# Modulation rows and summed blocks turned over on TensorE and added up by VectorE

## The reference, cut to what matters

```python
mod = silu(c) @ w_mod[l] + b_mod[l]              # 6 * 1024 values for each of two streams
sh1, sc1, g1, sh2, sc2, g2 = split(mod, 6)
h = rmsnorm(x, norm1_g) * (1 + sc1) + sh1        # first norm
y = token_mixing(h)                              # three mixers, gates, output projection
x = x + g1 * y
h = rmsnorm(x, norm2_g) * (1 + sc2) + sh2        # second norm
x = x + g2 * ec_moe(h)                           # 16 routed experts
```

## Time and profile before

| what | value |
|---|---|
| median of 3 runs | 1779.37 us (1778.21 to 1779.48) |
| span of the profiled execution | 1775.2 us |
| PE busy | 1694.8 us, 95% |
| DVE busy | 647.5 us, 36% |
| ACT busy | 290.4 us, 16% |
| HBM read | 530.76 MB, 300 GB/s over the span |

### The profile page before, as it was taken

One profiled execution on the slowest core, in us unless ns is written; L12 is line 12 of the kernel. 1 busy time (PEld: TensorE's weight loads), 2 busy tenths in 40 slices (PEclk: granted clock), 3 DMA queues, 4 the chain that ended last, 5 costly groups with the idle time before them and its releaser, 6 DMA issues.

```text
span 1775.2 us, 18819 instructions
## 1 busy us (share of the span) xinstructions
PE 1694.8 (95%) x7152; PEld 799.4 (45%) x7152; DVE 647.5 (36%) x1374; ACT 290.4 (16%) x736; POOL 118.6 (7%) x161
## 2 busy tenths in 40 slices
PE   7999999999999998898999999999999998988988
PEld 3456566654434332242345565666553433323322
DVE  1257656566122120121124566666661111211211
ACT  2234222002101010000022432221030100000100
POOL 0251000000000000000012500000000000000000
PEclk9999999999999999999999999999999999999999
DMA  9531333755999999999993223238559999999997
GB/s 396 184 119 48 117 118 114 284 237 198 411 427 428 429 428 429 427 430 426 426 366 126 101 95 114 102 115 331 216 222 413 426 428 429 428 429 428 428 428 328
DMA packets 49250, 533.81 MB, mean 301 GB/s; under 512 B 5856, under 2 KB 7040, under 8 KB 10528
## 3 DMA queue, kind: packets, MB, share of 16 engines
q1 hardware_dynamic: 45360, 522.74, 71.3%
q0 software_dynamic: 2112, 7.97, 1.3%
q10 hardware_dynamic: 1712, 2.20, 0.3%
HBM read 530.76 MB, written 2.13 MB: 300 GB/s over the span
## 4 chain that ended last, share of the span: by engine, by line
PE 75%; DMA 21%; DVE 2%; ACT 1%; issue 1%; SPq 0%; DVEq 0%
PE bank L2081 21%; DMA ring<-in_w_moe 21%; PE bank L1678 12%; PE bank L1697 7%; PE bank L1744 7%; PE bank L2118 5%; PE bank L1930 5%; PE bank L1784 2%; PE bank L1844 2%; PE bank L1997 1%; PE bank L1706 1%; PE bank L1819 1%; PE bank L1669 1%; PE bank L1666 1%; PE bank L1628 1%; PE bank L1868 1%
## 5 line engine op out<-in xcount | busy, mean ns | idle before, releaser
L1678 PE MATMUL bank<-hT,ring 128*128 128x384 f32 x768 | 258.2, 490 | 0.0
L2081 PE MATMUL bank<-M,hT 128*64 128x512 f32 x992 | 221.4, 595 | 16.6 <-DMA M<-in_w_moe 16.1
L2081 PE MATMUL bank<-ring,hT 128*64 128x512 f32 x1024 | 227.1, 594 | 10.1 <-DMA ring<-in_w_moe 10.1
L1678 PEld LDWEIGHTS bank<-hT,ring 128*128 128x128 f32 x768 | 143.6, 190 | 102.5 <-issue 6.7
L2081 PEld LDWEIGHTS bank<-ring,hT 128*64 128x64 f32 x1024 | 72.5, 137 | 156.2 <-issue 139.7
L2081 PEld LDWEIGHTS bank<-M,hT 128*64 128x64 f32 x992 | 69.9, 137 | 158.0 <-issue 133.9
L1697 PE MATMUL bank<-M,ring 128*128 128x384 f32 x384 | 134.4, 493 | 0.7 <-ACT M L792 0.7
L2081 PE MATMUL bank<-ring,M 128*64 128x512 f32 x512 | 115.4, 596 | 15.6 <-DMA ring<-in_w_moe 14.2
L2081 PE MATMUL bank<-M 128*64 128x512 f32 x512 | 115.9, 595 | 14.4 <-DMA M<-in_w_moe 14.4
L1744 PE MATMUL bank<-ring,hT 128*128 128x512 f32 (+1 forms) x288 | 117.4, 567 | 0.7 <-DVE hT L1111 0.7
L991 ACT ACTIVATE hT<-bank 128x512 f32<-128x512 f32 x32 | 19.1, 597 | 572.1 <-PE bank L2081 572.1
(11 more groups left out here) (242 smaller groups left out, 1535.7 us busy)
## 6 DMA issues: line engine op xcount, KB each, us to landing
ring<-in_w_moe SPq DMA_DIRECT2D x96, 2048.0 KB, 30.8
M<-in_w_moe SPq DMA_DIRECT2D x94, 2048.0 KB, 30.4
ring<-in_w_mix SPq DMA_DIRECT2D x110, 1024.0 KB, 5.1
arena<-in_w_moe SPq DMA_DIRECT2D x2, 2048.0 KB, 14.7
ring<-in_w_mix SPq DMA_DIRECT2D x4, 576.0 KB, 5.1
arena<-in_bias_rows POOLq DMA_DIRECT2D x4, 512.0 KB, 6.3
g2slot<-in_bias_rows POOLq DMA_DIRECT2D x4, 512.0 KB, 6.9
M<-in_counts POOLq DMA_DIRECT2D x2, 768.0 KB, 8.1
```

The source lines that it names most:

```text
L1678: ins = mm(ps[:, 0:TOK], w[:, q, (j % 4) * P:(j % 4 + 1) * P], hT[:, 4 * h + q, :], start=(h == 0 and q == 0), stop=(h == 1 and q == 3))
L2081: ins = mm(bank[b][64 * e:64 * e + 64, :], lhs(e, 4 * h + q), w[:, q, :], start=(h == 0 and q == 0), stop=(h == 1 and q == 3))
```

## The change

The matmul against `pair` and the matmul against a column of ones are both replaced by a transpose (against the identity) of the same 128 x 128 block; the sum over partial rows, now along the free axis of PSUM, is taken by VectorE.

- TensorE's `turn_row(l, i)` replaces `mod_cols`: four transposes of `row_of(i)` into a bank of its own, ("turned", i), at banks 2 and 3 for blocks 0 and 2, and 6 and 7 for blocks 1 and 3. VectorE's `total` reduces that bank: of each 128 turned values it takes four (32q + r), for two streams and four blocks of channels, 32 values into 8. This is done for the shift block and then for the scale block, each reduction followed by what was there before (the scale's bias now reads SBUF).
- TensorE's `column(i)` makes eight transposes: four for stream 0 into bank 5 and four for stream 1 into bank 4. VectorE's `column(i)` reduces each bank, 512 values into 4, and then adds the bias; for a scale the bias and the 1 are added by one instruction where there were two.
- The constant `pair` is gone (the first table is 128 columns instead of 130); GpSimd's load of the bias rows waits for the second stream's bank.

```diff
-    use(("modcol", 0), 2)
+    for k, i in enumerate((0, 2)):
+        use(("turned", i), 2 + k)
...
-    use(("modcol", 2), 6)
+    for k, i in enumerate((1, 3)):
+        use(("turned", i), 6 + k)
...
         if m in (2, 4, 6):
-            use(("col", 5 + m // 2), 5)
+            for v in range(2):
+                use(("col", 5 + m // 2, v), 5 - v)
...
-    use(("col", 9), 5)
+    for v in range(2):
+        use(("col", 9, v), 5 - v)
...
-            def mod_cols(l, k, name, lo, hi, count):
+            def mod_cols(l, k, first, second, lo, hi, count):
...
-                step(V.tensor_tensor(shift[k][:, lo:hi, :], v[:, 0:n, :], col(b0), ALU.add))
-                b, c = turn(l, ("modcol", name))
-                V.scalar_tensor_tensor(amp[k][:, lo:hi, :], v[:, n:2 * n, :], 1.0, col(b0 + KB), ALU.add, ALU.add)\
-                    .then_inc(bank_read[b], 1)
-                dve.wait_ge(bank_read[b], c + 1)
-                V.tensor_tensor(amp[k][:, lo:hi, :], amp[k][:, lo:hi, :], col(g0), ALU.mult).then_inc(cols_ready, 1)
+                def total(dst, i):
+
+                    ps = wait_full(dve, l, ("turned", i))
+                    read(l, ("turned", i), V.reduce_sum(dst, ps[:, :].rearrange("p (c q r) -> p c r q", q=4, r=32)[:, :, 0:2, :],
+                                                        axis=AX))
+                    wait_read(dve, l, ("turned", i))
+                move, gain = shift[k][:, lo:hi, :], amp[k][:, lo:hi, :]
+                total(move, first)
+                step(V.tensor_tensor(move, move, col(b0), ALU.add))
+                total(gain, second)
+                step(V.scalar_tensor_tensor(gain, gain, 1.0, col(b0 + KB), ALU.add, ALU.add))
+                V.tensor_tensor(gain, gain, col(g0), ALU.mult).then_inc(cols_ready, 1)
...
-                    read(l, ("col", i), V.tensor_tensor(dst, v, col(COL_B + 24 + (0 if i < 8 else KB)), ALU.add))
-                    wait_read(dve, l, ("col", i))
-                    if i >= 8:
-                        step(V.tensor_scalar(dst, dst, 1.0, None, ALU.add))
+                    for v in range(2):
+                        ps = wait_full(dve, l, ("col", i, v))
+                        read(l, ("col", i, v), V.reduce_sum(dst[:, :, v], ps[:, :].rearrange("p (c k) -> p c k", k=P), axis=AX))
+                        wait_read(dve, l, ("col", i, v))
+                    if i < 8:
+                        step(V.tensor_tensor(dst, dst, col(COL_B + 24), ALU.add))
+                    else:
+                        step(V.scalar_tensor_tensor(dst, dst, 1.0, col(COL_B + 24 + KB), ALU.add, ALU.add))
...
-            def mod_cols(l, k, i, j, last):
-
+            def turn_row(l, i):
+
+                ps = begin(l, ("turned", i))
                 wait_read(pe, l, ("mod", i))
-                ps = bank[turn(l, ("modcol", k))[0]]
                 for c in range(4):
-                    ins = mm(ps[:, 8 * j + 2 * c:8 * j + 2 * c + 2], row_of(i)[:, c * P:(c + 1) * P], pair,
-                             start=True, stop=True)
+                    ins = turn_over(ps[:, c * P:(c + 1) * P], row_of(i)[:, c * P:(c + 1) * P], ident)
...
-                    ps = begin(l, ("col", i))
                     pe.wait_ge(mod_summed, 2 * len(SUMMED) * l + SUM_AT[i, 1])
-                    for s in range(2):
+                    for v in range(2):
+                        ps = begin(l, ("col", i, v))
                         for c in range(4):
-                            ins = mm(ps[:, 2 * c + s:2 * c + s + 1], part_sum(i, s)[:, c * P:(c + 1) * P], ones[:, 0:1],
-                                     start=True, stop=True)
-                    done(l, ("col", i), ins)
+                            ins = turn_over(ps[:, c * P:(c + 1) * P], part_sum(i, v)[:, c * P:(c + 1) * P], ident)
+                        done(l, ("col", i, v), ins)
```

More of the change, by code:

```diff
@@ L42 @@
 ROW_QG, ROW_KG, ROW_QCG, ROW_KVG, ROW_MQG, ROW_MKG, ROW_SINK, NROW = 0, 64, 128, 512, 768, 864, 960, 968
-_sizes = [("ident", P), ("pair", 2), ("ones", P), ("slots0", P), ("slots1", P), ("fold", NE),
+_sizes = [("ident", P), ("ones", P), ("slots0", P), ("slots1", P), ("fold", NE),
           ("slotno", 2 * SLOTS), ("band", 2 * P), ("ropes", 2 * 2 * SD), ("ropem", 2 * 2 * ROPE)]
@@ L51 @@
 NCONST = _at
-NFIRST = P + 2
+NFIRST = P
 def const_table():
@@ L68, in const_table @@
         put(f"slots{k}", np.repeat((stream == k)[None, :], P, 0))
-    put("pair", np.stack([r % 32 == 0, r % 32 == 1], 1))
     put("fold", (r[:, None] % 32 == np.arange(NE)[None, :]))
@@ L379, in hybrid_step @@
         stream_slots = (cst_("slots0"), cst_("slots1"))
-        pair = cst_("pair")
         fold = cst_("fold")
@@ L680, in _ @@
                 for n, i in enumerate(BIASED):
-                    wait_full(pool, l, ("col", 8 + n) if n < 2 else ("modb", BIASED[n - 2], 1))
+                    wait_full(pool, l, ("col", 8 + n, 1) if n < 2 else ("modb", BIASED[n - 2], 1))
                     dst = modrow[:, :, :].rearrange("p s c -> p (s c)") if i % 2 == 0 else g2slot[:, :]
@@ L1078, in normalise @@
                 V.tensor_scalar(xn[:, t, :], x[:, t, :], rstd[:, t:t + 1], None, ALU.mult).then_inc(xn_ready, 1)
-            def mod_cols(l, k, name, lo, hi, count):
+            def mod_cols(l, k, first, second, lo, hi, count):
                 dve.wait_ge(cols_in, 16)
-                ps = wait_full(dve, l, ("modcol", name))
                 n = hi - lo
-                v = ps[:, 0:4 * n].rearrange("p (b s) -> p b s", s=2)
                 b0, g0 = COL_B + 24 * k, (COL_N1, COL_N2)[k]
@@ L1180, in _ @@
                         h_raw(l, kb)
-                mod_cols(l, 0, 0, 0, KB // 2, 1)
+                mod_cols(l, 0, 0, 2, 0, KB // 2, 1)
                 h_front(l)
@@ L1185, in _ @@
                         h_raw(l, kb)
-                mod_cols(l, 0, 2, KB // 2, KB, 2)
+                mod_cols(l, 0, 1, 3, KB // 2, KB, 2)
                 for kb in BACK[0::2]:
@@ L1314, in column @@
                 def column(i):
-                    ps = wait_full(dve, l, ("col", i))
-                    v = ps[:, 0:8].rearrange("p (c s) -> p c s", s=2)
                     lo = 4 * (i % 2)
@@ L1632, in mod @@
                         done(l, ("mod", i), ins)
-            def mod_cols(l, k, i, j, last):
+            def turn_row(l, i):
+                ps = begin(l, ("turned", i))
                 wait_read(pe, l, ("mod", i))
-                ps = bank[turn(l, ("modcol", k))[0]]
                 for c in range(4):
-                    ins = mm(ps[:, 8 * j + 2 * c:8 * j + 2 * c + 2], row_of(i)[:, c * P:(c + 1) * P], pair,
-                             start=True, stop=True)
-                if last:
-                    done(l, ("modcol", k), ins)
+                    ins = turn_over(ps[:, c * P:(c + 1) * P], row_of(i)[:, c * P:(c + 1) * P], ident)
+                done(l, ("turned", i), ins)
             def norm_turn(l, name, k, kbs):
@@ L1754, in _ @@
                 else:
-                    begin(l, ("modcol", 0))
-                    mod_cols(l, 0, 0, 0, False)
+                    turn_row(l, 0)
                 mod(l, 2)
                 if l == 0:
-                    begin(l, ("modcol", 0))
-                    mod_cols(l, 0, 0, 0, False)
-                mod_cols(l, 0, 2, 1, True)
+                    turn_row(l, 0)
+                turn_row(l, 2)
                 norm_turn(l, "h1", 0, FRONT)
@@ L1768, in _ @@
                 segment(1, 0, (0,))
-                begin(l, ("modcol", 2))
-                mod_cols(l, 2, 1, 0, False)
-                mod_cols(l, 2, 3, 1, True)
+                turn_row(l, 1)
+                turn_row(l, 3)
                 segment(1, 0, (1, 2))
```

## The result

The changed kernel takes 1768.71 us, median of 4 runs (1768.14 to 1768.98), against 1779.42 us of the kernel before: a ratio of 0.994, with a 95% interval of 0.9928 to 0.9952. That is 10.7 us or 0.6% faster.

A forecast was written before the change was run, and what follows sets the result against it. TensorE was taken to bound the work ahead of the experts, DMA the experts. Per layer: fronts 0, blocks 1 and 3 0.83, column 6 0.47, columns 7 to 9 2.49; 7.6 us in all, giving 1771.8 us, range 1769.3 to 1775.8.

The forecast's parts named there:

- What bounds the kernel: TensorE bounds the work ahead of the experts, DMA the experts; a microsecond saved ahead reaches the layer's end whole.
- The size of one saving: Eight transposes at 0.87 us replace 16 narrow records at 1.70 us: 0.83 us saved for each group.
- VectorE's price: A reduction of 512 PSUM values takes 0.70 us, 0.86 at most; a small one of the rows 0.20 with its gap.
- the strided row: Profile row of 256 values into 32 results with a stride, 583 ns, read as some 170 ns over the line.
- rival 2: Reductions grown longer: about 9.8 - 6R a layer, 0.2% slower from R = 1.93 us; chance 0.01 for its middle.
- m = 2: Attention step with column 6: transposes of the probabilities wait for bank 4 behind VectorE's reductions; 0.47 of 0.83 us left.
- The fronts: Blocks 0 and 2 at each layer's start: gain lost to a transfer in layer 0, to VectorE in layer 1; 0.
- the sum's last line: Span becomes 1767.6 us; with the 4.2 us that the median has over the span, 1771.8 us, 0.43% faster.
- rival 3: Transposes lower TensorE's clock; 11 us of such work makes it 0.2% slower; chance 0.04 together with the end of rival 2.

The follow-up runs named there:

- swapped kernel: The changed kernel with the banks of columns 6, 7 and 8 exchanged (stream 0 in bank 4, stream 1 in bank 5): 1768.39 us, ratio 0.994.
- rows alone: The kernel before with only the rows of blocks 0 to 3 turned over, the columns as before: 1777.32 us, ratio 0.999.
- before once more: The unchanged kernel before, run again with the span and clock of each run: 1779.52 us, ratio 1.0.

## Why the prediction was wrong, point by point

- **What bounds the kernel: right.** What was saved ahead of the experts reached their end: 4.37 us behind column 9 became 4.46 at the front of layer 1, and the DMA share of the chain stayed at 21%.
- **The size of one saving: right for the group itself, small by 0.09 with what follows it.** Eight transposes take 0.87 us, as forecast (238.44 to 239.31). But a group brought 0.90 to 0.96 us instead of 0.83. At m = 4 and in most others the branch behind the group is shorter too: from its start to the first load of `turn_probs` 2.35 us before and 2.26 now (241.72 to 244.07, 239.31 to 241.57). The term looked only at the group. Why the branch is shorter, the traces don't say. Over all ten groups the ledger has 8.4 us for the forecast's 7.6, and this is the largest part of the difference between 7.6 and 8.6 in the traces; the rest is the start of the program (0.14) and small steps in the experts.
- **VectorE's price: right.** The reductions last 0.69 us each (forecast 0.70), the small ones 0.19 (0.17, 0.20 with a gap). Two slips changed nothing: the strided row lies 160 ns over the line, not 170, and rival 2's terms add up to 9.7, not 9.8.
- **m = 2: right in its mechanism, its size partly by luck.** It was to wait 0.7 us for bank 4 and waited 0.51; it was to keep 0.47 us and kept 0.54. But from the first record of the column to the gate only 0.34 was kept (5.31 to 4.97). Another 0.10 lies ahead of it (the column starts 1.15 us earlier, with 1.05 won before) and 0.10 in the gate behind it, and the forecast had neither. That `merge` holds the gate as well was in the sum, and the swapped kernel showed that it is `merge` that decides.
- **The fronts: right.** Layer 1's first projection is where the step before it put it (4.46 us earlier, as the work ahead of it), and of layer 0's gain of 0.5 us (3.66 to 3.15) only 0.14 was left behind the transfer in the kernel with rows alone, where TensorE idled 0.27 us for it. The changed kernel's own trace could not show this: there a transfer that block 2's matmuls wait for landed later (their load behind it stands at 18.17, not at 17.82), and most of the gain was gone before.
- **The step that failed: the sum's last line.** "With the 4.2 us that the median has over this span" took the difference between the median and one profiled execution for time that lies around the span in every run. Only 2.05 us of it lies there. The other 2.1 us lie inside the span: they are what a run loses when TensorE falls to 1.2 GHz behind column 6, as in nearly every run but the profiled one, and the change takes this loss away. The same holds for the sentence on "some 4 us more" ahead of the prediction. The earlier trace rows show the clock of one execution, and the prediction read them as the kernel's. Its rival 3 then asked only whether transposes could lower the clock; that the matmuls which they replace might lower it already was nowhere among the cases. With the 8.6 us of the traces and 2.1 of clock the sum gives the measured 10.7, more than the 10.0 that the prediction called the most the change could give. Without this step the miss would have been 1.0 us, 1770.8, and inside the range.

The chances were at fault in the same way: the range's lower end held the two fronts and m = 2 but neither the 0.09 for each group nor anything for the runs that the profile didn't show.

## What to carry to other kernels

Hold the profiled span against the time of its own run, not against the median of others. Where some microseconds are left over, look at the spans and the clock of the other runs before you take them for a constant. A matmul with one or two columns costs what its weights cost to load (0.106 us a record here, and 64 columns took no longer). Turning the block over and adding on VectorE halves that cost if VectorE has idle time there; look which bank VectorE then holds and what is queued behind it. And where TensorE waits, don't put matmuls of one column right behind the wait: here it cost 2 us, and either removing the wait or widening the matmuls gave them back.

## What the runs showed of the hardware

- In 64 of 66 runs of the kernel before the mean granted clock of TensorE was under 1.000. Two traces (before once more, rows alone) show it fall from 2.4 to 1.2 GHz for some microseconds (1075.15 to about 1078.5 in the first) behind 0.67 us of idle, during or behind 16 records of one-column matmuls. The price was 1.7 us in the profiled place and 2.0 to 2.1 us in the medians. Both traces have it at m = 2 of layer 1 only, with the same stretch in layer 0 at full clock; runs with a mean clock of 0.998 suggest a second place, which no trace caught.
- The same records with 64 columns took hardly longer (1.80 against 1.78 us to the next step) and the clock stayed up in 11 of 11 runs. With one column but without the idle ahead it also stayed up in 11 of 11.
- Transposes of the same length behind 0.58 us of idle kept it up in 8 of 8 runs; in the kernel with doubled reductions, which has a second idle of 1.97 us shortly behind, two of five runs had a clock of 0.999, without a trace of where.
- A sum over 512 values of PSUM into 4, written to every second element of the result, took 0.69 us. That is what the line through the two maxima of the earlier trace rows gives for 512 values; a maximum of that size was not measured.
